# LayerNorm 1 of a hybrid decoder layer on the partition side: centred operands, square sums by a product with ones, W_out loaded once

## What is computed

```python
mix = jnp.concatenate([y_pool, y_ml], axis=-1).astype(x.dtype) @ w_out
x1 = _layer_norm(ALPHA * x + mix, ln1_g, ln1_b)
ff = jnp.square(jax.nn.relu(x1 @ w_ff1 + b_ff1)) @ w_ff2 + b_ff2
x2 = _layer_norm(ALPHA * x1 + ff, ln2_g, ln2_b)

def _layer_norm(x, g, b):
    mu = jnp.mean(xf, axis=-1, keepdims=True)
    xc = xf - mu
    var = jnp.mean(xc * xc, axis=-1, keepdims=True)
    return xc * lax.rsqrt(var + LN_EPS) * g + b
```

## Time and profile before

| | before |
|---|---|
| median of 3 runs | 1066.43 us (1066.04 to 1066.63) |
| span of the profiled execution | 1064.2 us |
| TensorE busy | 1053.9 us |
| VectorE, ScalarE, POOL busy | 724.6, 500.3, 92.3 us |
| DMA moved | 139.9 MB, mean 131 GB/s |

### The profile page before, as it was taken

How to read it: one execution, slowest core, us unless ns; L and a number is a source line. 1 busy time by engine, 2 the same in 40 slices (tenths; PEclk the granted TensorE clock), 3 DMA queues, 4 the chain that set the end, 5 groups by cost and what they waited for, 6 DMA issues and landing times. The chain is left out here.

```text
span 1064.2 us, 19251 instructions
## 1 busy us (share of the span) xinstructions
PE 1053.9 (99%) x7935; PEld 1042.0 (98%) x7935; DVE 724.6 (68%) x989; ACT 500.3 (47%) x733; POOL 92.3 (9%) x119
## 2 busy tenths in 40 slices
PE   9999999999999999999999999999999999999996
PEld 9999999999899999999999999999999999999985
DVE  6795555537789864955555555558767577788977
ACT  6453535442554666654555545556452322334223
POOL 3010000020212320000000000000000000000027
PEclk9999999999999999999999999999999999999999
DMA  8502222362154841235435534568623525435304
GB/s 283 147 4 60 63 60 63 92 175 79 47 200 127 259 126 46 80 120 170 150 119 159 158 119 154 163 221 275 239 81 139 170 71 167 132 91 169 120 9 151
DMA packets 97394, 139.88 MB, mean 131 GB/s; under 512 B 5963, under 2 KB 56875, under 8 KB 96934
## 3 DMA queue, kind: packets, MB, share of 16 engines
q1 hardware_dynamic: 93728, 127.65, 37.9%
q0 software_dynamic: 3328, 10.77, 3.6%
q10 hardware_dynamic: 270, 0.49, 0.2%
HBM read 102.75 MB, written 36.38 MB: 131 GB/s over the span
## 5 line engine op out<-in xcount | busy, mean ns | idle before, releaser
L2201 PE MATMUL bank<-x_hi,w_hi 128*128 128x344 f32 (+1 forms) x696 | 228.1, 328 | 0.0
L2201 PE MATMUL bank<-x_hi,d_lo 128*128 128x258 f32 x968 | 222.4, 282 | 0.0
L2201 PE MATMUL bank<-x_lo,w_hi 128*128 128x344 f32 (+1 forms) x696 | 222.0, 319 | 0.0
L2201 PE MATMUL bank<-x_hi,w_lo 128*128 128x344 f32 x528 | 168.8, 320 | 0.0
L2201 PEld LDWEIGHTS bank<-x_hi,d_lo 128*128 128x128 f32 x968 | 165.7, 189 | 0.0
L2201 PEld LDWEIGHTS bank<-x_hi,w_hi 128*128 128x128 f32 (+1 forms) x696 | 130.4, 187 | 0.1
L2201 PEld LDWEIGHTS bank<-x_lo,w_hi 128*128 128x128 f32 (+1 forms) x696 | 130.3, 187 | 0.1
L2201 PE MATMUL bank<-x_lo,s_hi 128*128 128x258 f32 x448 | 126.5, 282 | 0.0
L2201 PE MATMUL bank<-x_hi,s_hi 128*128 128x258 f32 x448 | 126.4, 282 | 0.0
L2201 PEld LDWEIGHTS bank<-x_hi,w_lo 128*128 128x128 f32 x528 | 99.2, 188 | 0.0
L2201 PE MATMUL bank<-t_hi,s_hi 128*128 128x258 f32 x336 | 95.2, 283 | 0.0
(11 more groups left out here) (391 smaller groups left out, 2485.2 us busy)
## 6 DMA issues: line engine op xcount, KB each, us to landing
h_ops<-h_unit SPq DMA_DIRECT2D x56, 258.0 KB, 2.8
x_lo_raw<-h_ops SPq DMA_DIRECT2D x14, 1032.0 KB, 5.3
s_raw<-in_w_ff SPq DMA_DIRECT2D x14, 1024.0 KB, 7.0
w_raw<-in_w_out SPq DMA_DIRECT2D x12, 1024.0 KB, 6.9
x_lo_raw<-h_ops SPq DMA_DIRECT2D x14, 774.0 KB, 4.5
d_raw<-in_w_ff SPq DMA_DIRECT2D x9, 1024.0 KB, 7.8
w_raw<-in_w_in SPq DMA_DIRECT2D x16, 512.0 KB, 6.2
h_ops<-t_out SPq DMA_DIRECT2D x28, 258.0 KB, 5.0
```

The costliest lines, as they stand in the source:

```text
L2201: return nc.tensor.matmul(out, lhsT, rhs, start=start, stop=stop, skip_group_check=True)
```

## The change

- x centred: the gate product gets one more column of -1/1024, so that its row 68 is minus the mean of each token (`GL[4]`, written to DRAM as `nm_d`). SP writes the high part of x^T to DRAM (`xt_d`), POOL adds the low part and minus the mean to it by accumulating DMAs between attention pairs 7 and 11; SP reads it back chunk by chunk into four slots (`XTM`).
- W_out centred: POOL loads W_out's rows in pairs after pairs 2 to 5, VectorE sums each row (`w_out_rows`), and ScalarE adds minus the row's mean to each unit in place (`centre`) before it is split. The mean over the features of ALPHA x + mix is then zero without being taken.
- W_out loaded once: the chains run in `OUT_ORDER` (unit, block): (0,0), (1,0), (0,1), (1,1), (0,2), (1,2), (2,0), (3,0), (2,1), (3,1), (2,2), (3,2), two chains each.
- LayerNorm 1 with features on the partitions: VectorE reads each chain's bank and adds ALPHA times the centred x (`residual`). ScalarE squares (`square`), VectorE sums the squares of six and then of two chunks (`sum_squares`), one float32 product with ones (`square_sums`) sums over partitions and spreads the sum, then root, reciprocal and two half products by 1/std (`normed`), gain, bias and high part (`x1_half`), low part (`x1_lo_half`). No token tile is transposed. `x1_lo` is waited for block by block in two halves.
- ScalarE waits for the last adding DMA before it writes the first heads' part over x (`cat_hi_part(0, True)`).

VectorE's order in the stage is then: residual(0); cat_lo_part(1, True); residual(1); q_times_C(0); cat_lo_part(1, False); residual(2); q_times_C(1); residual(3); q_times_C(2); residual(4); q_times_C(3); residual(5); cat_lo_part(2, False); residual(6); sample_rows(); residual(7); cat_lo_part(2, True); residual(8); new_C(0); residual(9); split_lo(U_OUT + 2); residual(10); new_C(1); residual(11); split_lo(U_OUT + 3); residual(12); residual(13); residual(14); sum_squares(0, False); residual(15); sum_squares(0, True); residual(16); r_std(0); residual(17); normed(0, 0); normed(0, 1); residual(18); sum_squares(1, False); residual(19); sum_squares(1, True); x1_lo_half(0, 0); residual(20); x1_lo_half(0, 1); r_std(1); residual(21); normed(1, 0); normed(1, 1); ffn_lo(0); residual(22); sum_squares(2, False); residual(23); sum_squares(2, True); x1_lo_half(1, 0); ffn_lo(1); r_std(2); normed(2, 0); normed(2, 1); x1_lo_half(1, 1); x1_lo_half(2, 0); x1_lo_half(2, 1).

The functions `mix_T`, `norm_T`, `ln1_a`, `ln1_b`, `mix_evac`, `ln1_sqrt`, `x1_T`, `norm1` and their calls are taken out. The rest of the diff, cut to its core:

```diff
-U_FFN = U_OUT + NBLK * (D // UW)
+U_FFN = U_OUT + D // UW
+OUT_ORDER = [(0, 0), (1, 0), (0, 1), (1, 1), (0, 2), (1, 2), (2, 0), (3, 0), (2, 1), (3, 1), (2, 2), (3, 2)]
...
+        XTM = at("x_T_centred", [P, 4, NT], R["h_blk"])
+        SQ = at("squares", [P, 9, BLK], R["qkv0"] - 3 * XROW)
+        SSQ = at("square_sum", [P, BLK], R["sample_C"])
+        RSTD = at("r_std", [P, BLK], R["square_sum"])
+        WR = [at(f"w_out_rows{x}", [P, D], o_r1 + (6 + x) * XROW) for x in range(2)]
...
+                if u == 3:
+                    sp.wait_ge(x_hi, 2 * len(XT) + 1 + NBLK)
+                    sp.dma_start(nm_d, GL[NH:NH + 1, 0, :]).then_inc(nm_out, 16)
                 if u >= 3:
                     load_rows(u - 3)
+                if u == 4:
+                    sp.dma_start(xt_d[:, 4:8, :], XH[:, 4:8, :].bitcast(F32)).then_inc(xt_hi, 16)
+                elif u == 5:
+                    for b in (0, 2):
+                        sp.dma_start(xt_d[:, 0:4, blk(b)], XH[:, 0:4, blk(b)].bitcast(F32)).then_inc(xt_hi, 16)
+                    sp.wait_ge(b12_out, 48)
+                    sp.dma_start(xt_d[:, 0:4, blk(1)], b12_d[0]).then_inc(xt_hi, 16)
...
+            def load_xt(m):
+                if m == 0:
+                    sp.wait_ge(xt_done, XT_DONE)
+                    sp.wait_ge(pooled, 4)
+                elif m == 1:
+                    sp.wait_ge(sn_out, 16)
+                elif m == 2:
+                    sp.wait_ge(E_ready, 2 * NPAIR)
+                    sp.wait_ge(qi_ready, NPAIR)
+                elif m == 3:
+                    sp.wait_ge(mixed, 12)
+                else:
+                    sp.wait_ge(gemm_read, outputs_of(m - 4, m - 3, NBLK - 1))
+                sp.dma_start(XTM[:, 3 - m % 4, :], xt_d[:, m, :]).then_inc(xt_in[m % 4], 16)
+
+            for j in range(D // UW):
+                u = U_OUT + j
                 sp.wait_ge(lo_done, u - 1)
                 sp.dma_start(wslot(RAW, u), w_out_v[:, :, UW * j:UW * (j + 1)]).then_inc(raw_in[u % 2], 16)
+                if j == 2:
+                    for m in range(4):
+                        load_xt(m)
...
+                    p = PAIRS * h + j
+                    if 2 <= p < 6:
+                        if p == 2:
+                            pool.wait_ge(dve_row, ROW_RX)
+                            pool.wait_ge(act_row, 6)
+                        else:
+                            pool.wait_ge(wr_sum, 2 * (p - 2))
+                        for x in range(2):
+                            k = 2 * (p - 2) + x
+                            pool.dma_start(WR[x][:, :], a["w_out"][0, P * k:P * (k + 1), :]).then_inc(wr_in, 16)
+                    elif p == 7:
+                        pool.wait_ge(xt_hi, XT0 + 64)
+                        pool.dma_start(xt_d[:, 4:8, :], XL[:, 4:8, :].bitcast(F32), max_dma_last_dim=4 * NT, accum_op=ALU.add).then_inc(xt_done, 16)
+                    elif p == 8:
+                        for b in (0, 2):
+                            pool.dma_start(xt_d[:, 0:4, blk(b)], XL[:, 0:4, blk(b)].bitcast(F32), max_dma_last_dim=4 * NT, accum_op=ALU.add).then_inc(xt_done, 16)
+                        pool.dma_start(xt_d[:, 0:4, blk(1)], b12_d[1], max_dma_last_dim=4 * NT, accum_op=ALU.add).then_inc(xt_done, 16)
+                    elif p in (10, 11):
+                        if p == 10:
+                            pool.wait_ge(nm_out, NM0 + 16)
+                            pool.wait_ge(xt_done, XT_LO)
+                        for k in range(4 * (p - 10), 4 * (p - 10) + 4):
+                            pool.dma_start(xt_d[:, k, :], nm_d.to_broadcast([P, NT]), max_dma_last_dim=4 * NT, accum_op=ALU.add).then_inc(xt_done, 16)
...
-            pool.wait_ge(nat_out, 16 * 7)
-            for t in range(len(TILES)):
-                for x in ((0, 1) if t == 0 else (t + 1,)):
-                    if x < len(TILES):
-                        if x >= 2:
-                            pool.wait_ge(res_done, x - 1)
-                        token_dma(pool, XN[0:TILES[x][1], x % 2, :], a["x_prompt"], a["x_sample"], x, True, xn_in[x % 2])
-                norm1(pool, t)
-                if t in (1, 2):
-                    store_C(t - 1)
-
-            pool.wait_ge(res_done, len(TILES))
+            for x in range(2):
+                store_C(x)
...
+            def centre(j):
+
+                u = U_OUT + j
+                act.wait_ge(raw_in[u % 2], RAW_AT[u])
+                if j == 0:
+                    act.wait_ge(wr_sum, KC + 1)
+                for k in range(KC):
+                    A(wslot(RAW, u)[:, k, :], wslot(RAW, u)[:, k, :], ACT.Identity, bias=WM[:, k:k + 1]).then_inc(w_centred, 1)
...
+                    act.wait_ge(xt_done, XT_DONE)
...
+                if u == 6:
+                    act.wait_ge(wr_sum, KC + 1)
...
+                    if (u, i) == (9, 4):
+                        centre(0)
+                    elif (u, i) == (10, 1):
+                        centre(1)
...
+            cat_hi_part(1, True)
+            cat_hi_part(1, False)
+            cat_hi_part(2, False)
+            centre(2)
+            cat_hi_part(2, True)
+            split_hi(U_OUT + 2)
+            centre(3)
+            split_hi(U_OUT + 3)
...
+            def square(b, last):
+                m0, m1 = (6, 8) if last else (0, 6)
+                act.wait_ge(gemm_read, outputs_of(m0, m1, b))
+                if not last:
+                    if b == 0:
+                        act.wait_ge(c_out, 128)
+                    else:
+                        act.wait_ge(sq_sum, 2 * b)
+                A(SQ[:, m0:m1, :], Y[:, m0:m1, blk(b)], ACT.Square).then_inc(squared, 1)
+
+            def root(b):
+                act.wait_ge(var_ready, VAR0 + b + 1)
+                if b:
+                    act.wait_ge(ln_norm, 2 * b)
+                A(RSTD[:, :], D_[:, 0:BLK], ACT.Sqrt, scale=1.0 / D, bias=EPSC).then_inc(ln_sqrt, 1)
+
+            def x1_half(b, h):
+                act.wait_ge(ln_norm, 2 * b + h + 1)
+                ks = slice(4 * h, 4 * h + 4)
+                for f in range(4 * h, 4 * h + 4):
+                    A(Y[:, f, blk(b)], Y[:, f, blk(b)], ACT.Identity,
                       scale=CST[:, G1 + f:G1 + f + 1], bias=CST[:, B1 + f:B1 + f + 1]).then_inc(xv_ready, 1)
+                act.wait_ge(xv_ready, KC * b + 4 * h + 4)
+                A(XH[:, ks, blk(b)], Y[:, ks, blk(b)], ACT.Copy).then_inc(x1_hi, 1)
+
+            square(0, False)
+            square(0, True)
+            root(0)
+            square(1, False)
+            x1_half(0, 0)
+            x1_half(0, 1)
+            square(1, True)
+            root(1)
+            ffn_hi(0)
+            square(2, False)
+            x1_half(1, 0)
+            square(2, True)
+            ffn_hi(1)
+            root(2)
+            x1_half(1, 1)
...
+            def w_out_rows(u, i):
+                if u in (4, 5) and i in (2, 5):
+                    for x in range(2):
+                        k = 4 * (u - 4) + 2 * (i // 3) + x
+                        dve.wait_ge(wr_in, 32 * (k // 2 + 1))
+                        V.tensor_reduce(WM[:, k:k + 1], WR[x][:, :], AX.X, ALU.add).then_inc(wr_sum, 1)
+                    if (u, i) == (5, 5):
+                        dve.wait_ge(wr_sum, KC)
+                        V.tensor_scalar(WM[:, :], WM[:, :], -1.0 / D, None, ALU.mult).then_inc(wr_sum, 1)
...
+            def residual(p):
+                j, b = OUT_ORDER[p // 2]
+                m, n = 2 * j + p % 2, N_PROJ + p
+                dve.wait_ge(gemm_done, n + 1)
+                if b == 0:
+                    dve.wait_ge(xt_in[m % 4], XT0 + 16 * (m // 4 + 1))
+                stt(Y[:, m, blk(b)], XTM[:, 3 - m % 4, blk(b)], ALPHA, bank[n % 3][:, 0:BLK], ALU.mult, ALU.add)\
+                    .then_inc(gemm_read, 1)
...
+            def sum_squares(b, last):
+                dve.wait_ge(squared, SQ0 + 2 * b + 1 + last)
+                if last:
+                    dve.wait_ge(sq_sum, 2 * b + 1)
+                    if b:
+                        dve.wait_ge(var_ready, VAR0 + b)
+                out, rows = (SSQ[:, :], slice(6, 9)) if last else (SQ[:, 8, :], slice(0, 6))
+                V.tensor_reduce(out, SQ[:, rows, :].rearrange("p m n -> p n m"), AX.X, ALU.add).then_inc(sq_sum, 1)
+
+            def r_std(b):
+                dve.wait_ge(ln_sqrt, b + 1)
+                V.reciprocal(RSTD[:, :], RSTD[:, :]).then_inc(ln_rstd, 1)
+
+            def normed(b, h):
+                dve.wait_ge(ln_rstd, RSTD0 + b + 1)
+                r = Y[:, 4 * h:4 * h + 4, blk(b)]
+                V.tensor_tensor(r, r, over_blocks(RSTD[:, :], 4), ALU.mult).then_inc(ln_norm, 1)
...
+            def square_sums(b):
+                pe.wait_ge(sq_sum, 2 * b + 2)
+                if b:
+                    pe.wait_ge(ln_sqrt, b)
+                else:
+                    pe.wait_ge(nat_read, 2)
+                mm(D_[:, 0:BLK], ONES[:, :], SSQ[:, :]).then_inc(var_ready, 1)
...
```

(129 more changed lines are left out.)

189 lines of the change are left out of this document (49 added, 140 removed).

## The result

The changed kernel takes 1076.51 us (median of four runs, 1076.08 to 1078.26), the kernel before 1066.51 beside it: ratio 1.0098, 95% interval 1.0084 to 1.0113. It is slower, where I had forecast 1056.1 us and a range of 1052.6 to 1061.0. The profiled execution has a span of 1075.0 us against 1064.2.

The account below looks back on a forecast made before the run. TensorE, busy 1053.9 of 1064.2 us, was taken to bound the kernel. Terms of -15.6 + 2.3 + 1.9 + 0.6 + 0.5 = -10.3 us took 1066.4 to 1056.1 us; forecast 1053 to 1057.5, wider range 1052.6 to 1061.

Parts of the forecast that it names:

- the sum: Whole kernel: transposes -15.6, ones products +2.3, stalls +1.9, reciprocals +0.6, late loads and adjacent stalls +0.5, together -10.3 us.
- The failed step: Additions on POOL's queue, 163 to 274 us: at 112 GB/s the low parts are in before 205; no cost.
- The rival of slow adding: POOL waits for the low parts, making mask 11 and attention late below 82 GB/s; 1069 to 1090 us, chance 0.08.
- The sum's 1.9 us of stall: Output projection: TensorE waiting for VectorE, all stalls together, with reductions at 1.3 ns an element.
- my upper end of 1.75: VectorE's strided reductions in the output projection: at 1.75 ns an element the stalls sum to 4.7 us.
- my layout: Output projection: VectorE, ScalarE and TensorE laid out in program order with semaphores; four places come near TensorE.
- two rows: Reduction rows of the old trace: contiguous 0.96 ns an element, strided inside 1.7 ns; 1.3 taken.
- The rival for it: VectorE's last chain of steps bounds the output projection: strided reductions at 1.75 ns, slow reciprocals; 1059 to 1060 us, chance 0.14.
- the transposes gone and what they were worth: LayerNorm 1 on TensorE: eighteen groups of eight transposes removed, all on the path, -15.6 us.
- the stall of 0.2 us ahead of chain 8: Output projection, unit 0 block 2: TensorE waits 0.2 us for `cat_lo` 6, which stands behind `residual(7)`.
- ones products: Output projection on TensorE: three full float32 products, 0.56 to 0.82 us each, 0.75 taken, +2.3 us.
- The first W_out row load: Projection units 4 and 5: row loads 0 to 3 us late for VectorE's reductions; 0.5 us taken in all.

Follow-up runs that it names:

- the run with written low parts: Against the kernel with the minus-mean additions moved to masks 13 and 14, the four transfers of x's low parts write instead of adding: 1062.08 us, a single run.
- the means late: Against the changed kernel, the eight additions of the minus-mean row move from masks 10 and 11 to masks 13 and 14: 1063.62 us, ratio 0.9969.
- repaired kernel: Against the changed kernel, minus-mean additions at masks 13 and 14 and strided reductions replaced by additions of whole rows: 1055.26 us, run again 1055.41 us.
- means in the middle: Against the changed kernel, the additions of the minus-mean row start one mask later, at masks 11 and 12: 1075.41 us, ratio 1.0078.
- half late: Against the changed kernel, only the second four additions of the minus-mean row move, to mask 13; the first four stay at mask 10: 1063.05 us, ratio 0.9964.

## Why the prediction was wrong, point by point

Of the 21.1 us between the forecast change of the span (-10.3) and the measured one (+10.8), 13.8 lie ahead of the output projection (it begins 14.9 us later, forecast 1.1), 6.8 in it (147.5 us, where the sum makes it 140.6) and 0.5 behind it.

*The failed step is the one that priced the additions.* I asked of 8.4 MB of additions only whether they would be done when POOL waited for them. The low parts were: slow adding was real (half the rate, by the run with written low parts), but POOL never waited. The sum has no term for what the additions do to other transfers, and that was the 11.7 us wait for the `x_lo` reload and the clock behind it. I did not ask who else needs the engines. I wrote that other transfers fit "unless adding is slow" and looked at 0.22 of use in 100 to 125 us, the stretch of the W_out rows, not at 200 to 250 us, where the additions of the means stand and where the kernel before already shows 0.87. There SP's reload, the row broadcasts, the sample states and the last weight units follow each other, each with TensorE behind it. Priced that way, with the durations measured since, it reads: eight transfers of 516 KB at 12 us for four are 24 us of full engines from 204 us on, with a reload issued at 209 and wanted at 229 in the middle. That marks the danger; the size of the wait doesn't follow from it, since how the engines share out their time isn't settled. The rival of slow adding had the right cause with the wrong victim, and a chance of 0.08; that its 1069 to 1090 us takes in the measured time is luck.

*Mis-sized term: the reductions.* The sum's 1.9 us of stall came out as 6.2. I took 1.3 ns an element; the six-chunk ones measured 2.3, past my upper end of 1.75, and behind the three stalls, of 6.2 us together, came 1.5 us of clock. Of these 6.2 about 2.2 needed the store of the sample states as well: I had no term for that wait, and my layout, in which ScalarE "lags nowhere", missed it. I had most of the stall ahead of the last ones product; the first got 2.61 us of it. Of two rows I trusted the contiguous one because there were more of its kind, though the new reductions stride and the strided row was the only one that did. Neither row gives the length: at the same stride the reduction over three chunks took 1.3 ns an element and the one over six 2.3, so the stride alone isn't it, and why six cost so much more stays open. The Trainium skill's advice against `tensor_reduce` ("VectorE: DVE Perf Modes", "Rules for kernel authors"), which I cited as speaking against the change, holds here: 3.3 us of additions do the work of 6.1. The rival for it gave 5 to 6 us of stalls and 1059 to 1060 us; with the means late, and so this loss alone, the kernel takes 1063.6. Its trace has 6.8 us of stalls and, by the length of the stage, some 2.9 us of low clock, which I had left out of every stall.

*Right:* the transposes gone and what they were worth, shown by the 140.1 us of the stage once both losses are out (forecast 140 to 141); the reciprocal at 2.30 us, by the row, not the 2.9 estimated from the repeat count in the Trainium skill ("VectorE: DVE Perf Modes", "First, the fixed hardware budget"); `residual` at 0.50; the stall of 0.2 us ahead of chain 8; ones products at 0.58 to 0.69 by the distance of starts, with the slow step behind each, in my 0.56 to 0.82 and under the 0.75 taken; the centring and splits on ScalarE covered. The first W_out row load was late for VectorE by 0.7 us and 0.5 us of that reached TensorE in unit 4, the size that I had taken for it; with all else repaired the stage begins 0.3 to 0.8 us later than before, where I had 1.1. The repaired kernel's 1055.3 to 1055.4 us against the 1056.1 of the sum fits its other terms, though errors in single terms could cancel in it. It is not what was asked, and the sum left out what made the sign.

## What to carry to other kernels

A transfer that nobody waits for still has a price: give every added DMA its engine time, lay it over the busy share of its own stretch in the old trace, and list each transfer issued within that backlog together with its slack to its reader. Then place it where that list is empty; here the same bytes 40 us later were worth 13 us. List every wait of each engine that feeds the critical one, stores included: a wait that is covered today may not be when the step behind it grows. For each stall near TensorE add what the clock may take behind it, and where no row has the shape of a strided reduction, price it with a wide margin or write it as additions of whole rows.

## What the hardware showed that I had not expected

- An adding transfer from SBUF to DRAM holds the engines twice as long as a plain write of the same 560 packets (11.5 against 5.4 us for 2.18 MB).
- A transfer can be held back by others issued after it: the `x_lo` reload of 210.1 took 30.5 us with four additions issued at 217.8, and 14.4 us without them (issued at 209.8 there), four earlier additions standing ahead of it both times.
- A reduction over six rows at a stride of 344 elements takes 2.3 ns an element, one over three 1.3 ns, an addition of whole rows 1.2 ns (1229 ns for 1032) to 1.5 (517 ns for 344). The first two have the same stride.
- The length of a TensorE stall of 2.5 to 3.2 us doesn't tell whether the granted clock falls behind it. It fell to 0.50 for 3.4 us behind one of 2.61 (changed kernel) and for 5.6 us behind one of 3.24 (late means), and stayed at 1.00 behind one of 2.51 (means in the middle). Behind the last ones product's stall of 2.97 us, the same in all of them, it stayed at 1.00 in the changed kernel and with late means, and fell with means in the middle (0.60 over the next 3 us) and half late (0.64 over 4.7 us). No run here shows why.
